# Normalised rows stored in contiguous blocks, and expert biases added by a picking matmul

## What is computed

```python
h = layer_norm(ALPHA * x + mix, ln1_g, ln1_b)                 # [256, 2048]
logits = h @ w_router + b_router                              # [256, 32]
top_w, top_idx = softmax over the 4 largest logits of each token
for each expert e, for the tokens routed to it (rows xb of h):
    gate = minimum(xb @ w_gate[e] + b_gate[e], 7)             # [*, 512]
    up   = clip(xb @ w_up[e] + b_up[e], -7, 7)
    y    = (gate * sigmoid(1.702 * gate) * (up + 1)) @ w_down[e] + b_down[e]
ffn = sum over the experts of top_w * y
out = layer_norm(ALPHA * h + ffn, ln2_g, ln2_b)
```

## Time and profile before

| | us |
|---|---|
| median of 3 runs | 3278.82 |
| lowest, highest | 3273.98, 3283.41 |
| profiled execution, device time | 3282.47 |
| its span | 3280.6 |
| TensorE busy in it | 3042.0 (93%) |
| TensorE weight loads busy | 2258.1 (69%) |
| VectorE busy | 957.1 (29%) |
| ScalarE busy | 476.9 (15%) |
| moved by transfers | 662.19 MB, mean 202 GB/s |

### The profile page before, as it was taken

How to read it: one execution, slowest core, us unless ns; L and a number is a source line. 1 busy time by engine, 2 the same in 40 slices (tenths; PEclk the granted TensorE clock), 3 DMA queues, 4 the chain that set the end, 5 groups by cost and what they waited for, 6 DMA issues and landing times.

```text
span 3280.6 us, 48447 instructions
## 1 busy us (share of the span) xinstructions
PE 3042.0 (93%) x19571; PEld 2258.1 (69%) x19571; DVE 957.1 (29%) x2650; ACT 476.9 (15%) x628; POOL 102.6 (3%) x194
## 2 busy tenths in 40 slices
PE   8999999999999896886969999958999999999995
PEld 7888888888888785776868888835455445445542
DVE  2342442442343064745630000031112111111214
ACT  2122122122121202011100000000111101111111
POOL 2100100100100000000000000000000000000000
PEclk9999999999999897988989999958999999999998
DMA  6234223224245341422324446526999999999994
GB/s 188 84 98 129 89 94 129 92 91 129 96 100 157 113 129 49 132 73 83 112 75 151 151 153 230 205 65 242 409 408 404 397 408 408 394 409 407 398 404 191
DMA packets 326069, 662.19 MB, mean 202 GB/s; under 512 B 41856, under 2 KB 271360, under 8 KB 275456
## 3 DMA queue, kind: packets, MB, share of 16 engines
q1 hardware_dynamic: 325920, 659.85, 54.7%
HBM read 657.73 MB, written 2.10 MB: 201 GB/s over the span
## 4 chain that ended last, share of the span: by engine, by line
PE 64%; issue 16%; DVE 9%; DVEq 4%; ACT 2%; ACTq 1%; POOL 1%; POOLq 1%; SPq 1%; DMA 0%
PE bank L950 13%; PE bank L831 10%; PE bank L595 9%; PE bank L939 7%; PE bank L981 7%; PE bank L852 3%; PE bank L997 3%; DVE arena L1519 2%; DVE arena L1521 2%; DVEq L1518 2%; PE bank L811 2%; PE bank L655 1%; PE bank L664 1%; PE bank L778 1%; PE bank L668 1%
## 5 line engine op out<-in xcount | busy, mean ns | idle before, releaser
L595 PE MATMUL bank<-arena 128*128 128x256 f32 x4096 | 937.1, 384 | 0.0
L595 PEld LDWEIGHTS bank<-arena 128*128 128x128 f32 x4096 | 770.0, 191 | 114.0 <-issue 7.7
L950 PE MATMUL bank<-arena 128*64 128x512 f32 x2048 | 442.2, 592 | 0.7 <-ACT arena L1219 0.7
L950 PEld LDWEIGHTS bank<-arena 128*64 128x64 f32 x2048 | 146.9, 137 | 292.8 <-issue 291.1
L831 PE MATMUL bank<-arena 128*128 128x256 f32 x1536 | 333.3, 380 | 7.4 <-ACTq L1174 7.4
L831 PEld LDWEIGHTS bank<-arena 128*128 128x128 f32 x1536 | 292.9, 191 | 47.8 <-issue 7.7
L939 PEld LDWEIGHTS bank<-arena 128*128 128x128 f32 x1024 | 224.7, 311 | 15.4 <-issue 12.2
L981 PE MATMUL bank<-arena 128*64 128x512 f32 x1024 | 224.9, 597 | 7.7 <-ACT arena L1229 7.7
L939 PE MATMUL bank<-arena 128*128 128x128 f32 x1024 | 227.8, 384 | 3.1 <-DVEq L1718 3.1
L796 PE MATMUL bank<-arena 128*128 128x256 f32 x1024 | 222.3, 379 | 0.0
L796 PEld LDWEIGHTS bank<-arena 128*128 128x128 f32 x1024 | 194.6, 190 | 26.5
(11 more groups left out here) (289 smaller groups left out, 2318.2 us busy)
## 6 DMA issues: line engine op xcount, KB each, us to landing
arena<-in_w_in_dram SPq DMA_DIRECT2D x72, 2048.0 KB, 8.7
arena<-in_w_gate_dram SPq DMA_DIRECT2D x64, 2048.0 KB, 16.9
arena<-in_w_up_dram SPq DMA_DIRECT2D x64, 2048.0 KB, 13.2
arena<-in_w_down_dram SPq DMA_DIRECT2D x64, 2048.0 KB, 19.2
arena<-in_w_dn_out_dram SPq DMA_DIRECT2D x16, 2048.0 KB, 8.6
arena<-in_w_glu_a_dram SPq DMA_DIRECT2D x8, 2048.0 KB, 8.5
arena<-in_w_glu_b_dram SPq DMA_DIRECT2D x8, 2048.0 KB, 8.4
arena<-in_w_mix_out_dram SPq DMA_DIRECT2D x8, 2048.0 KB, 8.4
```

Source lines behind the costliest of these rows:

```text
L595: last = mm(ps[bank][:, ct * T:ct * T + T], ring[:, buf, k, ct * P:ct * P + P], rhs[:, k, :], start=k == 0, stop=k == KD - 1)
L950: last = mm(ps[bank][CAP * o:CAP * o + CAP, :], xg[:, 4 * q + k, CAP * o:CAP * o + CAP], w[:, o, k], start=q == 0 and k == 0, stop=q == 3 ...
```

## The change

Two edits are made together, and a third comes with them.

1. `h1` is stored as `[p, m, k, q]` where channel `c = q*16 + k`. Block k is then 128 neighbouring elements of a partition. The gather reads `h1[:, m, 4*b + k]`, the transposes for the router `h1[:, m, k]`. The first norm works on `acc` (which takes the place that `h1` had) and only its last operation, the add of the bias, writes into `h1`, with a step of 128 elements between neighbouring channels. At the end `h1` is read back with that step, and the result goes to `acc`, from which it is stored. Since the block order of the channels is new, `w_router` is read as `(p k) e`, 2 KiB in one piece for each partition in place of sixteen of 128 bytes.
2. The gate and up biases of all 32 experts are loaded once (`bias_gu`, 32 partitions), ahead of the loop. For each pair VectorE copies two columns of the identity into `pair_pick` (32x128), and TensorE starts the gate bank and the up bank each with one matmul `pair_pick` x `bias_gu`. The `expand` matmuls then add to it. The 64 transfers of biases, the wait for `brow_free` and the two bias adds on VectorE go. The clamps read the banks.
3. The dense branch, which doesn't run with these inputs, has its access patterns changed to match.

The diff, cut to what runs:

```diff
-        h1 = at(SH, MT, D)
-        acc = at(SH + 4096, MT, D)
+        acc = at(SH, MT, D)
+        h1 = at(SH + 4096, MT, KD, P)
...
-        pbrow = at(6144, 2, F_E)
+        bias_gu = at(6144, 2, F_E)
+        pair_pick = masks[0:N_E, P:2 * P]
...
-            sp.dma_start(h1, x[0].rearrange("(m p) d -> p m d", p=P)).then_inc(x_loaded, 16)
+            sp.dma_start(acc, x[0].rearrange("(m p) d -> p m d", p=P)).then_inc(x_loaded, 16)
...
-            def load_biases(i):
-                for o in range(2):
-                    for c, b in enumerate((b_gate, b_up)):
-                        sp.dma_start(pbrow[CAP * o:CAP * o + CAP, c],
-                                     b[ds(2 * i + o, 1)].rearrange("o n -> (o n)").partition_broadcast(CAP)).then_inc(brow_loaded, 16)
+            def load_biases():
+                for c, b in enumerate((b_gate, b_up)):
+                    sp.dma_start(bias_gu[0:N_E, c], b).then_inc(brow_loaded, 16)
...
-            sp.dma_start(wr, w_router.rearrange("(k p) e -> p k e", p=P)).then_inc(rt_loaded, 16)
+            sp.dma_start(wr, w_router.rearrange("(p k) e -> p k e", k=KD)).then_inc(rt_loaded, 16)
...
                 with sp.Fori(1, PAIRS) as i:
                     for j in range(PER_PAIR):
-                        if j == 2:
-                            sp.wait_ge(brow_free, i)
-                            load_biases(i)
                         reload_unit(j, i)
...
-                    last = tr(ps[i][:, j * P:j * P + P], h1[:, m, k * P:k * P + P], ident[:, :])
+                    last = tr(ps[i][:, j * P:j * P + P], h1[:, m, k], ident[:, :])
...
-                            last = mm(ps[4 + b][:, k * P:k * P + P], h1[:, m, 4 * b + k::KD],
+                            last = mm(ps[4 + b][:, k * P:k * P + P], h1[:, m, 4 * b + k],
...
                             last = mm(ps[bank][CAP * o:CAP * o + CAP, :], xg[:, 4 * q + k, CAP * o:CAP * o + CAP], w[:, o, k],
-                                      start=q == 0 and k == 0, stop=q == 3 and k == 3)
+                                      start=False, stop=q == 3 and k == 3, skip_group_check=True)
...
             def sgate(i):
                 pe.wait_ge(xg_taken, 4 * i + 4)
+                if isinstance(i, int) and i == 0:
+                    pe.wait_ge(brow_loaded, 32)
                 if not isinstance(i, int) or i > 1:
                     pe.wait_ge(sc_taken, 8 * i - 8)
+                for c in range(2):
+                    mm(ps[c][:, :], pair_pick, bias_gu[0:N_E, c], start=True, stop=False, skip_group_check=True)
                 expand(0, 0, i)
...
-            def norm(m, rows, n):
+            def by_row(v):
+                return v.rearrange("p (q k) -> p q k", k=KD)
+
+            def in_blocks(m):
+                return h1[:, m].rearrange("p k q -> p q k")
+
+            def norm(m, rows, n, dst):
...
-                V.tensor_tensor(h1[:, m], h1[:, m], rows[:, 1], ALU.add)
+                V.tensor_tensor(dst, by_row(acc[:, m]), by_row(rows[:, 1]), ALU.add)
...
+                V.tensor_copy(pair_pick.rearrange("p (o c) -> p o c", o=2),
+                              ident[0:N_E, ds(2 * i, 2)].unsqueeze(2).to_broadcast([N_E, 2, CAP]))
                 dve.drain()
                 dve.sem_inc(p_built, 1)
...
-                dve.wait_ge(brow_loaded, 64 * i + 64)
-                V.tensor_tensor(sgb, ps[0][:, :], pbrow[:, 0], ALU.add)
-                dve.drain()
-                V.tensor_scalar(sgb, sgb, LIMIT, None, ALU.min)
+                V.tensor_scalar(sgb, ps[0][:, :], LIMIT, None, ALU.min)
...
-                V.tensor_tensor(shb, ps[1][:, :], pbrow[:, 1], ALU.add)
+                V.tensor_scalar(shb, ps[1][:, :], LIMIT, -LIMIT, ALU.min, ALU.max)
...
-                dve.sem_inc(brow_free, 1)
-                V.tensor_scalar(shb, shb, LIMIT, -LIMIT, ALU.min, ALU.max)
-                dve.drain()
...
-                V.scalar_tensor_tensor(out=h1[:, m], in0=h1[:, m], scalar=ALPHA, in1=acc[:, m], op0=ALU.mult, op1=ALU.add)
-                dve.drain()
-                norm(m, ln2row, MT + m)
+                V.scalar_tensor_tensor(out=by_row(acc[:, m]), in0=in_blocks(m), scalar=ALPHA, in1=by_row(acc[:, m]),
+                                       op0=ALU.mult, op1=ALU.add)
+                dve.drain()
+                norm(m, ln2row, MT + m, by_row(acc[:, m]))
```

More of the change, by code:

```diff
@@ L275, in build @@
         unit_read = [sem(f"unit{i}_free") for i in range(UNITS)]
-        brow_free = sem("brow_free")
         gate_done, gate_taken, up_done, up_taken = sem("gate_done"), sem("gate_taken"), sem("up_done"), sem("up_taken")
@@ L414, in load_gate @@
                 sp.dma_start(GW,
-                             w_gate[ds(e, 1)].rearrange("o (k p) n -> p (o k) n", p=P)).then_inc(gw_loaded, 16)
+                             w_gate[ds(e, 1)].rearrange("o (p k) n -> p (o k) n", k=KD)).then_inc(gw_loaded, 16)
             def load_up(e):
@@ L420, in load_up @@
                 sp.dma_start(UW,
-                             w_up[ds(e, 1)].rearrange("o (k p) n -> p (o k) n", p=P)).then_inc(uw_loaded, 16)
+                             w_up[ds(e, 1)].rearrange("o (p k) n -> p (o k) n", k=KD)).then_inc(uw_loaded, 16)
             def load_down(e):
@@ L432, in _ @@
             load_unit(UNITS - 1, 0)
-            load_biases(0)
+            load_biases()
             sp.dma_start(ln2row[:, 0], ln2_g.partition_broadcast(P)).then_inc(ln2_loaded, 16)
@@ L449, in _ @@
                     sp.wait_ge(unit_loaded[j], 16)
-                sp.wait_ge(brow_loaded, 64)
+                sp.wait_ge(brow_loaded, 32)
                 load_gate(0)
@@ L466, in _ @@
                 sp.wait_ge(out_ready, m + 1)
-                sp.dma_start(out[0, m * P:m * P + P, :], h1[:, m]).then_inc(out_done, 16)
+                sp.dma_start(out[0, m * P:m * P + P, :], acc[:, m]).then_inc(out_done, 16)
             sp.wait_ge(out_done, 32)
@@ L1574, in take_mix @@
                 dve.wait_ge(bank_ready[r % 3], use)
-                hv = h1[:, :, cols]
+                hv = acc[:, :, cols]
                 V.scalar_tensor_tensor(out=hv, in0=hv, scalar=ALPHA, in1=ps[3 + r % 3][:, :].rearrange("p (m n) -> p m n", m=2),
@@ L1586, in _ @@
             dve.wait_ge(ln_loaded, 32)
-            def norm(m, rows, n):
+            def by_row(v):
[3 more added lines that the diff above has]
+            def norm(m, rows, n, dst):
                 for i in range(4):
-                    V.bn_stats(stats[:, 6 * i:6 * i + 6], h1[:, m, 512 * i:512 * i + 512])
+                    V.bn_stats(stats[:, 6 * i:6 * i + 6], acc[:, m, 512 * i:512 * i + 512])
                 dve.drain()
@@ L1596, in norm @@
                 dve.wait_ge(ln_act, n + 1)
-                V.tensor_scalar(h1[:, m], h1[:, m], stats[:, 49:50], stats[:, 50:51], ALU.subtract, ALU.mult)
+                V.tensor_scalar(acc[:, m], acc[:, m], stats[:, 49:50], stats[:, 50:51], ALU.subtract, ALU.mult)
                 dve.drain()
-                V.tensor_tensor(h1[:, m], h1[:, m], rows[:, 0], ALU.mult)
+                V.tensor_tensor(acc[:, m], acc[:, m], rows[:, 0], ALU.mult)
                 dve.drain()
-                V.tensor_tensor(h1[:, m], h1[:, m], rows[:, 1], ALU.add)
+                V.tensor_tensor(dst, by_row(acc[:, m]), by_row(rows[:, 1]), ALU.add)
                 dve.drain()
             for m in range(MT):
-                norm(m, lnrow, m)
+                norm(m, lnrow, m, in_blocks(m))
             dve.sem_inc(h1_ready, 1)
@@ L1677, in take_gate @@
                 dve.wait_ge(gate_done, e + 1)
-                dve.wait_ge(brow_loaded, 32 * e + 96)
+                dve.wait_ge(brow_loaded, 32 * e + 64)
                 for m in range(MT):
```

## The result

| | before | changed |
|---|---|---|
| median of 4 runs, us | 3277.87 | 3221.47 |
| lowest, highest | 3273.98, 3283.41 | 3217.15, 3222.84 |
| profiled execution, us | 3282.47 | 3221.16 |
| its span, us | 3280.6 | 3219.3 |

The ratio is 0.9824, with a 95% interval of 0.9807 to 0.9842. The changed kernel gains 56.4 us by the medians and 61.3 by the profiled executions. Predicted were 68.2 off the profiled execution and 3210.6 us for the median: the time is 10.9 us above the forecast and inside the range, 3198 to 3236.

A forecast was written before the change was run, and what follows sets the result against it. TensorE was taken as the bound, 63.6 us a pair, moving to the unit stream at 59.5. 70.6 us gained less 2.4 at the end gave 68.2: 3278.8 - 68.2 = 3210.6 us, range 3198 to 3236.

The forecast's parts named there:

- The gather: Gather matmuls of each pair: with a contiguous stationary operand 64 rows at 111 ns, 7.1 us instead of 14.17.
- The picking matmuls: Bias matmuls ahead of gate and up: four rows of 0.43 us add 1.7 us a pair on TensorE.
- TensorE's own need: Expert loop: TensorE's work for a pair after the change, 63.6 - 7.1 + 1.7 = 58.2 us.
- The new bound: Expert loop: the stream of units, 59.5 us a pair, becomes the limit; TensorE's last 1.3 us turn into a wait.
- The rival of a slow stream: Expert loop: stream keeps only 405 GB/s, 5.178 us a unit, median 3250 us; chance 0.09.
- the biases' 2.3 us of the stream: Loop before the change: bias transfers, 0.52 MB a pair at 225 GB/s, take 2.3 us, making the stream 61.8 us.
- The first pair: Pair 0: gather 9.4 us, 4.9 less; pair_pick copy adds 0.2, bias matmuls 1.7; first released unit 3.0 us earlier.
- columns set the time: Bias matmuls: their 32 rows of depth buy nothing; the 512 columns give 0.43 us a row.
- Router and first norm: Ahead of the loop: w_router in 2 KiB pieces saves 1.4 us of the b_down wait; the norm's stepped writes cost nothing.
- the rival of the router's clock: Router matmuls: with b_down in time they start at full clock, 2.9 us wait and 6.9 matmuls less, 3201; chance 0.09.
- The tail: Last up unit to down matmuls: 9.8 us instead of 10.1, as VectorE's first up-bank operation shrinks from 692 to 428 ns.
- the end's reads: Two multiply-adds at the end read h1 with a step: 1.2 us more each, 2.4 us given back.

The follow-up runs named there:

- the last experiment: Changed kernel with 128-row picking matmuls, the residual ALPHA * h1 put into acc at the start, and weighted b_down formed inside pair 0: 3193.49 us, ratio 0.9744.

## Why the prediction was right

**The gather** came out as forecast: 7.34 us (7.1), at 115 ns a row. Its weight loads last 192 ns each, so the length of one load is not the pace of the rows.

**The picking matmuls** take 1.91 us a pair (1.7). In a stream-bound loop the 0.2 cost nothing. TensorE's own need was put at 58.2 us and is 58.85, so the slack is 0.8 and not 1.3; the order of the two bounds was right.

**The new bound** is where it was put: 59.66 us a pair (59.5), the last up unit waits for its transfer, and no slice of the loop is idle. The rival of a slow stream, 405 GB/s, is out: 422. But from the landing of the first reload, 2248.6, to that of the last up unit, 3149.4, are 900.8 us for 181 units, 4.977 each and not 4.958: 3.4 us more.

**Mis-sized, without harm to the forecast: the biases' 2.3 us of the stream.** That TensorE set the pace of before was right, and the experiment with the picking matmuls alone bears it out: 2 us more of TensorE, 2 us more for a pair. But the stream with biases was read as 61.8 us, 1.8 below TensorE, and once TensorE stops holding it back it needs 64.3. The working took the dip of two microseconds for the whole cost, in a stream that goes idle behind it; with units queued behind, the cost is twice that. That the forecast survived this is luck of the pairing: the change removes the biases too, and its floor was worked out from units alone. For the layout alone the same working gave 3252, where 3282.65 was measured.

**The first pair: expected at 2238.6, the first reload was issued at 2241.10.** TensorE's, ScalarE's and SyncE's timeline of the changed kernel, beside the earlier trace rows:

```profile
2223.02 10.08 PE L934 MATMUL bank<-arena 128*128 128x128 f32 x64 [3.20 <-DVEq L1725]
...
2233.77 2.13 PE L956 MATMUL bank<-arena,masks 32*128 32x512 f32 x4 [0.68 <-ACT arena L1218]
...
2235.83 7.73 PE L945 MATMUL bank<-arena 128*64 128x512 f32 x28
...
2241.10 0.38 SPq L392 DMA_DIRECT2D arena<-in_w_up_dram  x1
```

The gather takes 10.08 us (9.4 expected), the picks 2.13. The rest is a fall of the granted clock that no step of the forecast had:

```profile
2234.00:2236.00 2.00, 2.00 (x6) 0.60 (x7) 0.00 (x0) 1.02 (x1) 0.00 (x0) 0.87 0.00 0
2236.00:2238.00 2.00, 2.00 (x6) 0.60 (x8) 0.00 (x0) 0.00 (x0) 0.00 (x0) 0.50 0.00 0
2238.00:2240.00 2.00, 2.00 (x10) 0.56 (x8) 0.00 (x0) 0.00 (x0) 0.00 (x0) 0.78 0.00 0
```

From the first row of `expand` to the reload are 5.27 us, where before it was 2243.03 - 2239.26 = 3.77: 1.5 us for the fall. A short wait and the picking matmuls, of 32 rows, stand ahead of it. The prediction's "columns set the time" holds for their length and left out what their height does to the clock. The kernel without the picks, and the one with 128-row picks run twice, keep the clock at 1.00 at this place; the one with the picks alone loses it here too.

**Router and first norm: the sum held by luck, and two terms in it did not.** VectorE's last add of the norm is the stepped write, 2135 to 2225 us, and the multiply-add of the end the stepped read:

```profile
L1606 DVE TENSOR_TENSOR arena<-arena 128x2048 f32<-128x2048 f32 x2 | 7.3, 3632 | 0.2
```

```profile
L1782 DVE SCALAR_TENSOR_TENSOR arena<-arena 128x2048 f32<-128x2048 f32 x2 | 7.3, 3638 | 0.2
```

The read costs 1.35 us more than 2.29, the 1.2 of the forecast. But the write, which it put at nothing, costs the same 1.34, 2.7 for both blocks. The issue of `w_router` comes later, at 2164.34 in place of 2162.16. In return the bytes are there sooner than the 1.4 us allowed: from that issue to the router matmuls 10.55 us before and 8.25 now, 2.3 less. The two cancel, and the matmuls start at 2172.59, before it was 2172.71:

```profile
2172.59 12.52 PE L869 MATMUL bank<-arena 128*128 128x32 f32 x64 [3.20 <-DMA arena<-in_b_down_dram]
```

They take 12.52 us for 13.83, 1.3 less. Their first windows, 2172 to 2174 us, of before and after:

```profile
2172.00:2174.00 2.00, 1.29 (x7) 1.32 (x7) 0.00 (x0) 0.00 (x0) 0.00 (x0) 0.50 1.01 422
```

```profile
2172.00:2174.00 2.00, 1.41 (x13) 1.44 (x13) 0.00 (x0) 0.00 (x0) 0.00 (x0) 1.00 1.03 430
```

So the rival of the router's clock holds in part: with 3.20 us of waiting the clock is still full at their start, but it falls at 2174 and most of them run at the lower level. That rival had 6.9 us for the matmuls; 1.3 came. Its condition, `b_down` in time, was met in the last experiment, and the matmuls took 12.03 us: the clock falls under them even so.

**The tail.** Line 1736, the clamp on the up bank, takes 691 ns and not 428: what made's 428 was a source in SBUF, and this one reads the bank. The stretch to the down matmuls is 10.07 us (9.8).

**The accounts.** What the profiled execution fell short of the forecast, in us: the first reload 2.5 late, its landing 0.2 longer, the stream 3.4, the last up quarter and the tail 0.5, the end's reads 0.3. That is 6.9, the difference of 68.2 and 61.3. The other 4.9 us between 61.3 and the 56.4 of the medians are no step's: the profiled execution of before lay 4.6 above the median of its runs and that of after 0.3 below.

## What to carry to other kernels

Where two resources need nearly the same time, as 63.6 and 64.3 us for a pair here, relieving one alone gained nothing, and the dip in GB/s of a narrow transfer is to be read in a stretch where the stream doesn't go idle behind it. Spread transfers over 128 partitions: a share of 1.0 hides that 64 move half. Where a few small matmuls stand alone ahead of a chain, give them the full height of the array if the operands allow it, since here eight MATMUL rows of 512 columns took 3.63 us with 32 rows as with 128.

## What was not expected of the hardware

- Matmuls of 32 rows can lose the clock. Doubled, they let it fall to 1.2 GHz in most pairs (62.2 us a pair in the mean); the same with 128 rows keeps 1.00 in all (60.56). The 16 matmuls of `b_down`, 32 rows too, run 14.0 us without a pause at 0.50 and don't raise it, before as after, while it rises to 1.00 under the 128-row gather that follows a little later.
- Four transfers of 64 partitions, 0.52 MB, hold a stream of 422 GB/s back by 4.7 us when units are queued behind them; two of 128 partitions by 1.35.
- VectorE pays for a step in the write what it pays in the read: 3.63 us for 2048 float32 elements at 512 bytes apart, 2.29 contiguous. The Trainium skill (SBUF — State Buffer, section "Door 1: The DMA port swizzle") has SBUF in lines of 16 bytes, with a penalty for each access that crosses to a new one. The two 3.63 agree in direction. The prediction's estimate by it, in which a line for one element would halve VectorE, is too dear: the factor is 1.59.
